# Six levels in place of seven for the intra-chunk scores of a gated recurrence

## The reference

```
f    = lb + (1 - lb) * sigmoid(f_logit);  k = 1 - f;  logf = log(f)
bcum = cumsum(logf) inside the chunk
scores[t, s] = sum_c q[t, c] * k[s, c] * exp(bcum[t, c] - bcum[s, c])      for s <= t, else 0
o = scores @ v + (q * exp(bcum)) @ state
state = exp(btot) * state + (k * exp(btot - bcum))^T @ v
o = rms_norm(o, out_gain) * silu(g)
```

## Time and profile before

| | |
|---|---|
| median of 3 runs | 1180.26 us (1178.65 to 1181.34) |
| profiled execution | 1179.35 us |
| its span on the core | 1177.6 us |
| PE / PEld busy | 96% / 79% |
| DVE / ACT / POOL busy | 60% / 43% / 38% |
| chain that ended last, by engine | PE 77%, DVE 9%, POOL 4%, ACT 4%, issue 4% |
| share of L1393 in that chain | 4% |

### The profile page before, as it was taken

One profiled execution on the slowest core, in us unless ns is written; L12 is line 12 of the kernel. 1 busy time (PEld: TensorE's weight loads), 2 busy tenths in 40 slices (PEclk: granted clock), 3 DMA queues, 4 the chain that ended last, 5 costly groups with the idle time before them and its releaser, 6 DMA issues.

```text
span 1177.6 us, 14645 instructions
## 1 busy us (share of the span) xinstructions
PE 1124.7 (96%) x5540; PEld 927.3 (79%) x5540; DVE 701.6 (60%) x870; ACT 503.2 (43%) x773; POOL 443.8 (38%) x348
## 2 busy tenths in 40 slices
PE   7999999999999999876999999999999989999998
PEld 7988766788888788654888888888888867888876
DVE  7215598496878884669534232433333387778786
ACT  7314466535355521454333333333333355454531
POOL 0301134444242420302454545354544544352452
PEclk9999999999999999988899999999999989999999
DMA  7101100000005002400313332333223394545433
GB/s 268 36 4 52 36 19 19 21 34 22 34 18 185 26 1 94 179 19 18 126 63 117 116 117 58 112 134 102 98 87 116 145 331 167 161 134 177 132 99 149
DMA packets 37094, 112.65 MB, mean 96 GB/s; under 512 B 4896, under 2 KB 9760, under 8 KB 35616
## 3 DMA queue, kind: packets, MB, share of 16 engines
q1 hardware_dynamic: 37024, 111.71, 27.9%
HBM read 83.12 MB, written 28.57 MB: 95 GB/s over the span
## 4 chain that ended last, share of the span: by engine, by line
PE 77%; DVE 9%; POOL 4%; issue 4%; ACT 4%; DMA 2%; SPq 0%; DVEq 0%; ACTq 0%; POOLq 0%
PE ps L1211 23%; PE ps L1212 23%; PE ps L1213 23%; PE ps L1393 4%; PE ps L1352 1%; DVE olo L1838 1%; PE ps L1365 1%; PE ps L1227 1%; DVE B L1732 1%; POOL D L696 1%; DVE M L1765 1%; POOL sc L668 1%; DMA araw<-wd 1%; DMA ubraw<-hidden 1%; DVE h L1833 1%
## 5 line engine op out<-in xcount | busy, mean ns | idle before, releaser
L1211 PE MATMUL ps<-ubhi,adhi 128*128 128x512 f32 x308 | 121.7, 395 | 8.1 <-DVE yacc L1911 6.5
L1212 PE MATMUL ps<-ublo,adhi 128*128 128x512 f32 x308 | 120.8, 392 | 0.0
L1568 DVE TENSOR_TENSOR glo<-graw,ghi 128x1024 fp32r<-128x1024 f32 x21 | 26.8, 1276 | 147.3 <-POOL s34raw L615 147.3
L1211 PE MATMUL ps<-uhi,whi 128*128 128x512 f32 x272 | 112.1, 412 | 0.0
L1213 PE MATMUL ps<-uhi,wlo 128*128 128x512 f32 x272 | 106.4, 391 | 0.0
L1212 PE MATMUL ps<-ulo,whi 128*128 128x512 f32 x272 | 106.1, 390 | 0.0
L696 POOL TENSOR_TENSOR D<-B 128x1024 f32<-128x1024 f32 x28 | 64.2, 2293 | 42.2 <-DVE M L1765 22.9
L709 POOL TENSOR_TENSOR hst<-sg,up 128x512 f32<-128x512 f32 x21 | 27.9, 1327 | 132.8 <-issue 66.6
L1211 PE MATMUL ps<-ohi,s34hi 128*128 128x512 f32 x168 | 66.8, 398 | 10.5 <-ACT ps L1047 10.5
L1211 PEld LDWEIGHTS ps<-ubhi,adhi 128*128 128x128 f32 x308 | 58.5, 190 | 23.2 <-DVE yacc L1911 7.9
L1911 DVE TENSOR_TENSOR yacc<-ps,yacc 128x512 f32<-128x512 f32 x104 | 68.9, 682 | 10.9 <-PE ps L1213 10.7
(11 more groups left out here) (283 smaller groups left out, 3018.1 us busy)
## 6 DMA issues: line engine op xcount, KB each, us to landing
hidden<-hst SPq DMA_DIRECT2D x11, 1792.0 KB, 8.2
ubraw<-hidden SPq DMA_DIRECT2D x33, 512.0 KB, 5.2
graw<-wg SPq DMA_DIRECT2D x21, 512.0 KB, 4.2
uraw<-wu SPq DMA_DIRECT2D x21, 512.0 KB, 3.4
wraw<-wproj SPq DMA_DIRECT2D x17, 512.0 KB, 3.4
araw<-wd SPq DMA_DIRECT2D x22, 384.0 KB, 4.3
x<-xT SPq DMA_DIRECT2D x8, 512.0 KB, 6.7
h<-xT SPq DMA_DIRECT2D x8, 512.0 KB, 4.7
```

Source lines behind the costliest of these rows:

```text
L1211: nc.tensor.matmul(out, whi_, xhi_, start=first, stop=False, skip_group_check=seeded)
L1212: nc.tensor.matmul(out, whi_, xlo_, start=False, stop=False, skip_group_check=seeded)
L1568: nc.vector.tensor_tensor(glo[g % 2][:, :], graw[g % 2][:, :], ghi[g % 2][:, :].bitcast(F32), ALU.subtract)\
```

## The change

LEVELS becomes 6. The levels with L = 1 and L = 2 become one, which works on blocks of 4 tokens (BASE). Its reference is the mean of bcum at tokens 1 and 2 of the block, and its mask takes every pair s <= t of the block. The levels above keep their form, with L = 2^(lv + 1). For the mean, LV 0 on GpSimd gets two small instructions ahead of the subtraction, written to the first 256 columns of M0, with waits between them and a wait for M0 to be free. In the order, OX 1 comes a step earlier, and the last head's MS 6 and ML 6 stay at the step of index 5, which now is the last level's. The counts in all waits follow.

```diff
-LEVELS = 7
+LEVELS = 6
+BASE = 4
@@ schedule
-            steps[4] += [("OX", h - 1, 1)]
+            steps[3] += [("OX", h - 1, 1)]
-                for step in mix(take(n_p - taken[0]), steps[:6]):
+                for step in mix(take(n_p - taken[0]), steps[:LEVELS - 1]):
...
-                order += [("ML", 3)] + mix(take(TAIL), steps[6:])
+                order += [("ML", 3)] + mix(take(TAIL), steps[LEVELS - 1:])
@@ gpsimd, masks
-            for lv in range(LEVELS):
-                L = 1 << lv
+            base = lmask[:, 0, :].rearrange("p (b l) -> p b l", l=BASE)
+            step0(nc.gpsimd.memset(lmask[:, 0, :], 1.0))
+            step0(nc.gpsimd.affine_select(out=base, in_=base, compare_op=ALU.is_ge, fill=0.0, base=0,
+                                          pattern=[[-BASE, P // BASE], [0, BASE]], channel_multiplier=1))
+            step0(nc.gpsimd.affine_select(out=lmask[:, 0, :], in_=lmask[:, 0, :], compare_op=ALU.is_ge, fill=0.0,
+                                          base=0, pattern=[[1, P]], channel_multiplier=-1))
+            for lv in range(1, LEVELS):
+                L = 2 << lv
...
-            step0(nc.gpsimd.affine_select(out=lmask[:, 0, :], in_=lmask[:, 0, :],
-                                          compare_op=ALU.not_equal, fill=1.0, base=0, pattern=[[-1, P]],
-                                          channel_multiplier=1))
@@ gpsimd, LV
-                    L = 1 << lv
+                    L = 2 << lv
...
-                        pool.wait_ge(s_lvm, 2 * (7 * hh + lv - 1))
-                    b4 = B[:, :].rearrange("p (b l) -> p b l", l=2 * L)
-                    mid = b4[:, :, L - 1:L].broadcast_to([P, T // (2 * L), 2 * L])
-                    nc.gpsimd.tensor_tensor(DD[lv % 2][:, :].rearrange("p (b l) -> p b l", l=2 * L), b4, mid,
-                                            ALU.subtract).then_inc(s_lvs, 1)
+                        pool.wait_ge(s_lvm, 2 * (LEVELS * hh + lv - 1))
+                    if lv == 0:
+                        b4 = B[:, :].rearrange("p (b l) -> p b l", l=BASE)
+                        mid = M[0][:, 0:T // BASE]
+                        pool.wait_ge(*((s_lmm, 2 * LEVELS * hh) if hh else (s_tr, tr_count(2 * NC - 1))))
+                        nc.gpsimd.tensor_tensor(mid.unsqueeze(2), b4[:, :, 1:2], b4[:, :, 2:3], ALU.add).then_inc(s_mid, 1)
+                        pool.wait_ge(s_mid, 2 * hh + 1)
+                        nc.gpsimd.tensor_scalar(mid, mid, 0.5, None, ALU.mult).then_inc(s_mid, 1)
+                        pool.wait_ge(s_mid, 2 * hh + 2)
+                        nc.gpsimd.tensor_tensor(DD[0][:, :].rearrange("p (b l) -> p b l", l=BASE), b4,
+                                                mid.unsqueeze(2).broadcast_to([P, T // BASE, BASE]),
+                                                ALU.subtract).then_inc(s_lvs, 1)
+                    else:
+                        b4 = B[:, :].rearrange("p (b l) -> p b l", l=2 * L)
+                        mid = b4[:, :, L - 1:L].broadcast_to([P, T // (2 * L), 2 * L])
+                        nc.gpsimd.tensor_tensor(DD[lv % 2][:, :].rearrange("p (b l) -> p b l", l=2 * L), b4, mid,
+                                                ALU.subtract).then_inc(s_lvs, 1)
@@ the waits, on every engine
-                        act.wait_ge(s_lvm, 14 * hh)
+                        act.wait_ge(s_lvm, 2 * LEVELS * hh)
...
-                    act.wait_ge(s_lvs, 7 * hh + lv + 1)
+                    act.wait_ge(s_lvs, LEVELS * hh + lv + 1)
...
-                        pe.wait_ge(s_cp, 14 * hh)
+                        pe.wait_ge(s_cp, 2 * LEVELS * hh)
...
```

More of the change, by code:

```diff
@@ L356, in build @@
         s_kt, s_kte = sem("kd_t"), sem("kd_t_evac")
+        s_mid = sem("block_middle")
         s_lvs, s_lve, s_lvm, s_lmm, s_cp = sem("lv_sub"), sem("lv_exp"), sem("lv_mul"), sem("lv_product"), sem("lv_kept")
@@ L947, in _ @@
                     _, hh, lv = step
-                    L = 1 << lv
-                    act.wait_ge(s_lvs, 7 * hh + lv + 1)
+                    L = 2 << lv
+                    act.wait_ge(s_lvs, LEVELS * hh + lv + 1)
                     if lv == 0:
-                        act.wait_ge(*((s_lmm, 14 * hh) if hh else (s_tr, tr_count(2 * NC - 1))))
+                        act.wait_ge(*((s_lmm, 2 * LEVELS * hh) if hh else (s_tr, tr_count(2 * NC - 1))))
                         nc.scalar.activation(M[1][:, :], DD[0][:, :], ACT.Exp, scale=-1.0).then_inc(s_lve, 1)
-                        act.wait_ge(s_lve, 14 * hh + 1)
+                        act.wait_ge(s_lve, 2 * LEVELS * hh + 1)
                         nc.scalar.activation(DD[0][:, :], DD[0][:, :], ACT.Exp).then_inc(s_lve, 1)
@@ L1382, in _ @@
                     _, hh, lv = step
-                    pe.wait_ge(s_lvm, 2 * (7 * hh + lv + 1))
+                    pe.wait_ge(s_lvm, 2 * (LEVELS * hh + lv + 1))
                     lhs, rhs = (M[lv % 2], M[lv % 2]) if lv else (rec[:, hh, :], M[0])
@@ L1388, in _ @@
                     for c in range(NC):
-                        done = 2 * (7 * hh + lv - 1) + c // 4 + 1
+                        done = 2 * (LEVELS * hh + lv - 1) + c // 4 + 1
                         if c % 4 == 0 and lv:
@@ L1399, in _ @@
                     if c == 0:
-                        pe.wait_ge(s_cp, 14 * (hh + 1))
+                        pe.wait_ge(s_cp, 2 * LEVELS * (hh + 1))
                         pe.wait_ge(s_qi, hh + 1)
@@ L1720, in _ @@
                     if hh:
-                        dve.wait_ge(s_lvm, 14 * hh)
+                        dve.wait_ge(s_lvm, 2 * LEVELS * hh)
                     nc.vector.tensor_scalar(K[:, :], rawf[:, :], nomlb[:, hh:hh + 1], omlb[:, hh:hh + 1],
@@ L1747, in _ @@
                     _, hh, lv = step
-                    L = 1 << lv
-                    dve.wait_ge(s_lve, 2 * (7 * hh + lv + 1))
+                    L = 2 << lv
+                    dve.wait_ge(s_lve, 2 * (LEVELS * hh + lv + 1))
                     if lv == 0:
                         if hh:
-                            dve.wait_ge(s_lmm, 14 * hh)
+                            dve.wait_ge(s_lmm, 2 * LEVELS * hh)
                         nc.vector.tensor_tensor(M[0][:, :], Q[:, :], DD[0][:, :], ALU.mult).then_inc(s_lvm, 1)
@@ L1758, in _ @@
                     if lv == 1:
-                        dve.wait_ge(s_lvm, 14 * hh + 2)
+                        dve.wait_ge(s_lvm, 2 * LEVELS * hh + 2)
                     else:
-                        dve.wait_ge(s_lmm, 2 * (7 * hh + lv - 1))
+                        dve.wait_ge(s_lmm, 2 * (LEVELS * hh + lv - 1))
                     for up, src in ((0, K), (1, Q)):
@@ L1768, in _ @@
                     for x2 in range(2):
-                        dve.wait_ge(s_lmm, 2 * (7 * hh + lv) + x2 + 1)
+                        dve.wait_ge(s_lmm, 2 * (LEVELS * hh + lv) + x2 + 1)
                         if lv == 0 and x2 == 0:
@@ L1772, in _ @@
                         if lv:
-                            dve.wait_ge(s_cp, 2 * (7 * hh + lv - 1) + x2 + 1)
+                            dve.wait_ge(s_cp, 2 * (LEVELS * hh + lv - 1) + x2 + 1)
                         av = A[:, x2 * HALF:(x2 + 1) * HALF].rearrange("p (c t) -> p c t", t=P)
```

## The result

| | before | after |
|---|---|---|
| median of 8 runs each | 1179.52 us | 1183.51 us |
| lowest to highest | 1178.33 to 1181.34 | 1180.74 to 1186.92 |
| profiled execution | 1179.35 | 1184.05 |
| its span | 1177.6 | 1182.3 |

The ratio is 1.0031 with a 95% interval of [1.0018, 1.0044]: the change makes the kernel some 4 us slower. I had forecast 1178.5 us, a range up to 1181.9, and 13% for slower.

A forecast was written before the change was run, and what follows sets the result against it. The kernel was taken as bound by TensorE's queue. Head 0 -1.4, heads 1 and 2 together -1.0 and head 3 +0.7 gave -1.7 us; against the 1180.26 us median, 1178.5 us, range 1174.8 to 1181.9.

The forecast's parts named there:

- What TensorE is relieved of: Recurrent stretch: one level fewer per head, 1.80 us of TensorE each, -7.2 us over four heads.
- The delay d: LV 0 on GpSimd: sum 0.73, halving 0.43 and two gaps of 0.07 make the subtraction begin 1.3 us later.
- My own turning point: Total change of about 4d - 6.9 us, d being LV 0's delay; it turns to a loss at d = 1.7.
- rival (b): LV 0 takes the removed level's place: +2.4 us passed at d = 2.3, +8 at 1.9 per operation; chance 13%.
- That d arrives whole in heads 1 and 2: TensorE's wait for KDT before the first product grows from 0.76 to 2.06 us; each head -0.5 us net.
- The surcharge in head 3: VectorE's D<-K,D slips in between GpSimd's sum and halving, about 1.2 us on top of 1.3; head 3 +0.7 net.
- Head 0: Transposes wait less, VectorE sets the pace to level 3, which starts 0.9 us late; net -0.9 to -1.8, taken as -1.4.
- The granted clock is 1.00 in the stretch: TensorE's clock was read as 1.00 (2.4 GHz) in the recurrent stretch that the change touches; no clock loss was priced there.
- All further stages move as a block: Stages behind the recurrent stretch, output projection and feed-forward included, all shift by the same amount, waiting for semaphores, not a clock.

The follow-up runs named there:

- e1: Changed kernel without the two small GpSimd operations, token 1 serving as the block's middle, six levels kept; 1174.72 us, ratio 0.9949 to the kernel before.
- e6: Changed kernel with unused products of ones filling TensorE's idle time ahead of heads 1 and 2's first level and head 3's transposes; 1179.46 us, ratio 0.9997 to before.
- e7: Changed kernel with the two small operations moved from GpSimd to VectorE, behind its tail subtraction; 1177.16 us, ratio 0.9979 to the kernel before.
- e4: Changed kernel with two more dense parts laid ahead of the first level of heads 1, 2 and 3; 1187.62 us, ratio 1.0066 to the kernel before.
- a1_after: The changed kernel traced once more, unedited; recurrent stretch 206.51 us, the rest 762.13 us.
- e3: Changed kernel with the small sum reading packed columns and the subtraction taking token 1, so the small operations' result is unused; 1184.87 us, ratio 1.0037 to before.

## Why the prediction was wrong

**What TensorE is relieved of**: right. A level costs it 1.8 us; four are 7.2, and e1 gave 7.8 on like work, since head 0 is partly at VectorE's pace.

**The delay d**: the first step that failed, a term mis-sized. The sum was right (0.73 foreseen, 0.67 alone). The halving was put between a memset and an affine select, at 0.43, and takes 0.85; the subtraction with the middle in a tile of its own takes 2.0 in place of 1.9. So d is 1.8, not 1.3. My own turning point stood at 1.7: by my formula, 4d - 6.9, the right d gives +0.3, no gain, but still within the range. (The same formula makes the far end of rival (b), at d = 3.9, +8.7, not +8.)

**That d arrives whole in heads 1 and 2**: right. 0.76 + 1.8 = 2.55, measured 2.55 and 2.57.

**The surcharge in head 3**: the mechanism was right, the number by luck. D<-K,D did slip in ahead of the halving, and in head 0 too, where the transposes wait under 0.2 us in place of 1.4. The total of 2.65 for 2.5, and the stall of 4.9 for 4.7, come out because two errors cancel: d was 0.5 too small, and the surcharge, foreseen at 1.2, was 2.65 - 1.8 = 0.85.

**Head 0**: right, -1.4 foreseen, -1.5 measured (69.74 us from the first cut to head 1's transposes, 71.21 before). The small operations cost it 0.9 us: e1 takes 68.81.

**"The granted clock is 1.00 in the stretch"**: the step that put the time out of the range. I took the clock as a property of the stretch, and it follows what TensorE does in it. Stalls of up to 2.25 us had left it alone there; I forecast stalls of 2.06 and 4.7 and did not ask what they do. It cost 2.6 us (e6), more than the whole forecast change. Without it the recurrent stretch is 0.6 us shorter than before, on like work, against -1.7 foreseen, and the median, 1179.46 us in e6, lies within the range.

**"All further stages move as a block"**: failed in its precision. They vary by 4 us between executions of one kernel.

Together: 7.2 and 0.6 removed, 7.15 added by what the small operations do in the four heads (0.9, 1.8, 1.8 and 2.65), 2.6 by the clock, so +2.0 on like work, as measured. Of the 3.7 us between this and the forecast -1.7, 1.1 are the delay's and 2.6 the clock's. Rival (b), which the range held only in part, named the mechanism and the size of d from which it decides; what made its price real was the clock.

## What to carry to other kernels

Work taken out of the bounding engine's queue is worth its time only as long as nothing is put at the head of a chain for which that engine waits: two operations of under 1 us each cost 10 us, against a saving of 7.8. Where an edit lengthens a stall of TensorE, price the stall and then the clock after it, and look in the profile for the longest stall that has left the clock alone. It is no safe bound: 2.25 us left it alone here, and half clock followed 1.83 us in e7. To cover a stall by moving work, first read what else stands in the queues between (e4); to take it away, take the reason (e1: a reference that needs no computing).

## What the runs showed of the hardware

- A stall of 2.55 us was followed by half clock in head 1 and not in head 2 of the same execution, and in both in two others (a1_after, e3): whether the clock falls behind a given stall is not fixed. Behind 4.8 to 4.9 us in head 3 it fell in all six traces that have this stall, and behind 3.8 to 3.9 us in all three heads of e4. It also fell in e7 at 240.4 and 339.4, behind waits of 2.35 and 1.83 us, but not behind the same 1.83 us at 285.12, and not behind 2.3 us in e1. With the waits of heads 1 to 3 filled by unused products it stayed at 2.4 GHz through the recurrent stretch (e6, one trace).
- GpSimd's multiplication of 128x256 by a constant takes 0.85 us, its addition of two operands of that size 0.67 (e4); VectorE takes 0.29 for the first (e7).
- In these traces VectorE's and GpSimd's operations on two SBUF operands hold each other up for whole instructions, small ones too: a sum of 256 columns took 2.79 us on VectorE behind a GpSimd product, and 1.52 on GpSimd behind a VectorE one. GpSimd's halving, which has one operand, was held up as well: 1.71 to 1.73 us for 0.85.
